# Retention slots of a two-layer decoder step: key transposes and the sample tokens' matvecs moved from the slot's begin into the middle of its weight chunk

## The chip, the cores and the metric

The kernel runs on one NeuronCore of a Trainium2 chip. The metric is the device time of one execution in microseconds (us), as the median of several executions. The engines are TensorE (PE, with its weight loads shown apart as PEld), VectorE (DVE), ScalarE (ACT), GpSimd (POOL) and SyncE (SP), which issues the weight loads from HBM. A row's line, such as L1725, is a line of the kernel before.

## What is computed

A decoder step of two layers for 256 prompt tokens and 8 sample tokens (264 columns, T, in all), in float32. Each layer runs a gated short convolution and a retention branch beside each other, then a dense (layer 0) or a mixture-of-experts (layer 1) channel mixer. Retention, for each of 4 heads, in the form that matters here (q, k, v of 128 rows):

```python
scores = jnp.einsum('blhd,bmhd->bhlm', q, k) * decay[None]
intra = jnp.einsum('bhlm,bmhe->blhe', scores, v)
inter = jnp.einsum('blhd,bhde->blhe', q, state) * q_dec[None, :, :, None]
new_state = jnp.exp(L * log_gamma)[None, :, None, None] * state + jnp.einsum(
    'blhd,blhe->bhde', k * k_dec[None, :, :, None], v)
return intra + inter, new_state
...
a = (cb * conv_out) @ w_conv_out
r = (jax.nn.silu(g.astype(jnp.float32)) * o).astype(xn.dtype) @ w_ret_out
m = jax.nn.sigmoid(ga) * a + jax.nn.sigmoid(gr) * r
return m @ w_o, new_buf, new_state
```

The prompt has no old state; each sample token has its own, of 128 x 128 for each head.

## The kernel before

**Weight chunks.** All weights stream through one ring as chunks of 128 x 2048 floats. SP loads a chunk into `raw` (6 buffers) when the chunk six before it has been cast. ACT writes its rounded half `whi` (L792, 3 buffers) when the PE has begun the chunk behind the one whose buffer it takes, in a slot the slot's own chunk (`chunk_begun`), DVE writes the rest `wlo = raw - whi` (L1246) and releases SP. The PE forms a product as three matmuls (`whi*xh`, `whi*xl`, `wlo*xh`; L1725, L1728, L1729). In the stage at hand a chunk gives 4 output tiles of 12 matmuls (conv) or 2 tiles of 24 (gate), 48 matmuls in all. A tile lies in one of 3 PSUM banks (`RING`): the PE may start tile p when DVE has taken tile p-3 (`tile_taken`; L1429 for conv tiles, L1287 for gate tiles).

**Retention slots.** Behind the last input chunk a layer has ten slots (`for s in range(SLOTS)` on PE, ACT and DVE). Slot s handles a piece of the retention of head s (or s-1, s-2) and then one weight chunk: 2 conv chunks, then 8 gate chunks. In slot s the PE does in this order:

1. slots 1 to 4, head s-1: the outer product of the sample tokens' keys and values for 4 tokens, `outer(0)` (L1822, into bank 7); the prompt's state (L1827) and outputs (L1830, L1831; bank 5); `outer(1)` for the other 4 tokens. It waits for the tiles `ktok`, `kst` and `vd` of head s-1 (`ktok_ready`, `kst_ready`, `vtok_ready`), and `outer(1)` for the first half of the state update (`s_new`), since both use bank 7.
2. slots 0 to 3: two 128 x 128 transposes of the keys and one of the sample keys (L1841, L1842; bank 3). Slots 2 to 5: the 8 matvecs of the sample tokens of head s-2 with their new state (L1848, shown as 16 instructions). `bank3_ready` follows, once a slot.
3. slots 0 to 3: the transposes of the values (L1853, L1854) and the scores (L1855, L1856).
4. the slot's chunk (`chunk`).

Slots 6 to 8 have the normalization of the outputs in place of 1 to 3.

**ACT in a slot:** on `bank3_ready` the copies `ktok` (two, L854), `kst` and `kraw` (L856, L857), and the sample outputs (L860); the prompt's state and outputs (L863, L864); then the cast of a chunk two ahead (L792); from slot 3 on the sigmoids of two gate tiles of the slot before (L847, with a table load in slots 3 and 5), in slot 4 also a silu (L876).

**DVE in a slot:** `state(0)` (L1380; it waits for `outer(0)` and for the loaded old state, `s_in`); copies of the values (L1386, L1387, L1392), the rest of `kst` (L1390), the block-diagonal `vd` (L1396), the decayed scores (L1399, L1400), `state(1)` (L1380), the cast `wlo` (L1246), in slots 3 to 6 the gating of two tiles with ACT's sigmoids (`gated`, L1372), and last the takes of the slot's tiles.

**POOL:** the samples' old states lie in two buffers `St`. POOL stores head h's new state and then, for heads 2 and 3, loads the old state into a free buffer (L532) when `bank3_ready` says that slot h's matvecs are through with it.

Of the kernel before, what the change touches and what calls it, by code (L numbers as in the profile page):

```python
# [34 lines left out]
SEQ = 256  # L35
NB = 8
# [109 lines left out]
def program(nc, A, O):  # L146
# [4 lines left out]
    with es:  # L151
# [634 lines left out]
        def _(act):  # L786
# [37 lines left out]
            for l in range(DEPTH):  # L824
# [22 lines left out]
                        nc.scalar.activation(g, g, ACT.Sigmoid).then_inc(gsig, 1)  # L847

                for s in range(SLOTS):
                    if s < NH:  # L850
                        h = s
                        act.wait_ge(bank3_ready, 6 * l + s + 1)
                        for i in range(2):
                            nc.scalar.activation(ktok[:, 128 * i:128 * i + 128], PS[:, 3, 128 * i:128 * i + 128], ACT.Copy,  # L854
                                                 scale=kd[:, 2 * h + i:2 * h + i + 1]).then_inc(ktok_ready, 1)
                        nc.scalar.activation(kst, PS[0:24, 3, 256:384], ACT.Copy, scale=m1).then_inc(ktok_ready, 1)  # L856
                        nc.scalar.activation(kraw, PS[0:24, 3, 256:384], ACT.Copy).then_inc(kraw_ready, 1)  # L857
                    if 2 <= s < NH + 2:
                        act.wait_ge(bank3_ready, 6 * l + s + 1)
                        nc.scalar.activation(Qt[:, s - 2, SEQ:T], PS[:, 3, 384:384 + NB], ACT.Copy).then_inc(os_taken, 1)  # L860
                    if 1 <= s < NH + 1:
                        act.wait_ge(o_ready, 4 * l + s)
                        nc.scalar.activation(so[:, s - 1, :], PS[:, 5, 384:512], ACT.Copy).then_inc(so_ready, 1)  # L863
                        nc.scalar.activation(Qt[:, s - 1, 0:SEQ], PS[:, 5, 0:SEQ], ACT.Copy).then_inc(o_taken, 1)  # L864
                    if s == 6:
                        act.wait_ge(cent_ready, l + 1)
                        nc.scalar.activation(Qt, PS[:, 4:8, 0:T], ACT.Copy).then_inc(oc_ready, 1)
                    if s == 7:
                        act.wait_ge(var_ready, l + 1)
                        nc.scalar.activation(gstat[:, 0, :], PS[0:TT, 3, 0:12], ACT.Sqrt, bias=epsb[0:TT, :],  # L870
                                             scale=1.0 / DK).then_inc(groot_ready, 1)
                    cast(slot_chunk(b, s) + AHEAD)
                    if s > 2:
                        sigmoids(s - 1)
                    if s == 4:
                        nc.scalar.activation(Gt, Gt, ACT.Silu).then_inc(gsilu_ready, 1)  # L876
                    if s == 8:
                        act.wait_ge(r32, l + 1)
                        nc.scalar.activation(fr[:, 0:4 * T], Qt, ACT.Copy).then_inc(r_hi, 1)
# [353 lines left out]
        def _(dve):  # L1233
# [74 lines left out]
            for l in range(DEPTH):  # L1308
# [63 lines left out]
                        v.tensor_tensor(zt[:, n, :], zt[:, n, :], gate_tile(n), ALU.mult).then_inc(a_gated, 1)  # L1372

                for s in range(SLOTS):
                    if 1 <= s < NH + 1:
                        r = 4 * l + s - 1
                        def state(hf):
# [6 lines left out]
                    if s < NH:  # L1384
                        dve.wait_ge(vT_ready, 4 * l + s + 1)
                        v.tensor_copy(vtok, PS[:, 6, 0:256]).then_inc(vtok_ready, 1)  # L1386
                        v.tensor_scalar(vst, PS[0:24, 6, 256:384], m2, None, ALU.mult).then_inc(vst_ready, 1)  # L1387
                        dve.wait_ge(ktok_ready, 12 * l + 3 * s + 3)
                        dve.wait_ge(kraw_ready, 4 * l + s + 1)
                        v.tensor_tensor(kst, kraw, kst.bitcast(F32), ALU.subtract).then_inc(kst_ready, 1)  # L1390
                        dve.wait_ge(vst_ready, 8 * l + 2 * s + 1)
                        v.scalar_tensor_tensor(vst, PS[0:24, 6, 256:384], float(DK ** -0.5), vst.bitcast(F32),  # L1392
                                               ALU.mult, ALU.subtract).then_inc(vst_ready, 1)
                        dve.wait_ge(vst_ready, 8 * l + 2 * s + 2)
                        dve.wait_ge(kst_ready, 4 * l + s + 1)
                        v.tensor_tensor(vd, vst.bitcast(F32).unsqueeze(1).to_broadcast([24, 8, 128]),  # L1396
                                        eye24.unsqueeze(2).to_broadcast([24, 8, 128]), ALU.mult).then_inc(vtok_ready, 1)
                        dve.wait_ge(score_ready, 4 * l + s + 1)
                        v.tensor_tensor(sc[:, 0:256], PS[:, 4, 0:256], dec[:, s, :], ALU.mult).then_inc(sc_ready, 1)  # L1399
                        v.tensor_tensor(sc[:, 256:384], PS[:, 4, 256:384], dec[:, s, 0:128], ALU.mult).then_inc(sc_ready, 1)  # L1400
# [24 lines left out]
                    if s < 2:  # L1425
                        for j in range(4 * s, 4 * s + 4):
                            p = t["conv"] + j
                            dve.wait_ge(tile_ready, p + 1)
                            v.tensor_copy(zt[:, j, :], PS[:, p % RING, 0:T]).then_inc(tile_taken, 1)  # L1429
                    else:  # L1430
                        for n in (2 * s - 4, 2 * s - 3):
                            take(t["gate"] + n, gate_tile(n), rstd[:, :])

                def m_rest(j):
                    dve.wait_ge(m_hi, 8 * l + j + 1)
# [274 lines left out]
        def _(pe):  # L1710
# [17 lines left out]
                mm(out, wh, al, start=False, stop=False)  # L1728
                return mm(out, wl, ah, start=False, stop=last)  # L1729

            def chunk(c, p, nk, nt, ah, al, turns=0, turns12=0, each=None, norm=None):

                ready(c, turns)
                W = nt * 128
                for n in range(nt):
# [7 lines left out]
                    ins.then_inc(tile_ready, 1)  # L1743
                    if n == 0 and norm is not None:
                        stat(norm)

            def stat(norm):

# [29 lines left out]
            for l in range(DEPTH):  # L1778
# [26 lines left out]
                pe.wait_ge(kv_rows, 2 * l + 2)  # L1805
                pe.wait_ge(tile_taken, t["in"] + 24)
                for s in range(SLOTS):
                    if s > 0 and s <= NH:

                        h, r = s - 1, 4 * l + s - 1  # L1810
# [22 lines left out]

                        pe.wait_ge(s_new, 2 * r + 1)
                        outer(1)
                    if s < NH + 2:
                        if s > 2:
                            pe.wait_ge(os_taken, 4 * l + s - 2)
                        if s < NH:
                            for i in range(2):  # L1840
                                nc.tensor.transpose(PS[:, 3, 128 * i:128 * i + 128], Kt[:, s, 128 * i:128 * i + 128], ident)  # L1841
                            ins = nc.tensor.transpose(PS[0:24, 3, 256:384], sq[:, 24 * s:24 * s + 24], ident)  # L1842
                        if s >= 2:

                            r = 4 * l + s - 2
                            pe.wait_ge(s_new, 2 * r + 2)
                            for i in range(NB):
                                ins = mm(PS[:, 3, 384 + i:385 + i], St[r % 2][:, 128 * i:128 * i + 128],  # L1848
                                         Qt[:, s - 2, SEQ + i:SEQ + i + 1], start=True, stop=True)
                        ins.then_inc(bank3_ready, 1)  # L1850
                    if s < NH:
                        for i in range(2):
                            nc.tensor.transpose(PS[:, 6, 128 * i:128 * i + 128], Vt[:, s, 128 * i:128 * i + 128], ident)  # L1853
# [24 lines left out]
                    if s < 2:  # L1878
                        if s == 0:
                            pe.wait_ge(a_lo, l + 1)  # L1880
                        chunk(b["conv"] + s, t["conv"] + 4 * s, 4, 4, frt[:, 0:4, :], frt[:, 4:8, :])
                    else:
                        chunk(b["gate"] + s - 2, t["gate"] + 2 * s - 4, 8, 2, xht, xlt)
                pe.wait_ge(r_lo, l + 1)
                for i in range(2):
                    chunk(b["ret"] + i, t["ret"] + 4 * i, 4, 4, frt[:, 0:4, :], frt[:, 4:8, :])
# [65 lines left out]
```

## Time and profile before

| | us |
|---|---|
| median of 3 executions | 1825.89 |
| lowest, highest | 1825.65, 1826.80 |
| the profiled execution: device time | 1828.56 |
| the profiled execution: span of the core | 1826.80 |
| slots 0 to 9, layer 0 (first key transpose to last gate tile) | about 111 to 201 |
| slots 0 to 9, layer 1 | about 604 to 695 |

The profile page gives each engine's busy time, the chain of work that ended last, and groups of instructions. The timeline lists an engine's instructions in order of time: start, duration, engine, line, operation, and in brackets how long the engine had been idle before and what released it. Consecutive equal instructions are merged, with the time from the first's start to the last's end. A PE matmul's duration includes its latency, so in a stream the starts tell the pace.

### The profile page before, as it was taken

How to read it: one execution, taken by the hardware profiler on the slowest of the kernel's cores; microseconds unless marked ns; L12 is line 12 of the kernel's file. 1: busy time of each engine (PE TensorE's matmuls, PEld its weight loads, DVE VectorE, ACT ScalarE, POOL GpSimd, SP SyncE). 2: the span in 40 equal slices, each digit the busy share in tenths (PEclk: the TensorE clock that was granted, in tenths of full speed). 3: DMA queues.
4: the chain of work that ended last, by engine and by line, in shares of the span. 5: the costliest groups of instructions: out<-in, count | busy, mean ns of one | idle time of the engine just before them, and what ended most of it. 6: DMA issues, size and time to landing. Idle time of an engine off the chain costs nothing.

```text
span 1826.8 us, 27978 instructions
## 1 busy us (share of the span) xinstructions
PE 1765.9 (97%) x10593; PEld 1568.5 (86%) x10593; DVE 1440.2 (79%) x1341; ACT 1072.5 (59%) x877; POOL 148.2 (8%) x157
## 2 busy tenths in 40 slices
PE   5999999999989999899999999999999999999987
PEld 5989999999989899778888888888888888888866
DVE  5786676556678766588898988988988989989886
ACT  3334544444443255477777777777777777767753
POOL 3112220000231123100000000000000000000002
PEclk9999999999999999799999999999999999999998
DMA  9555455655654545299999999999999999999950
GB/s 294 190 167 171 157 175 167 196 187 144 206 184 163 173 150 168 71 357 374 330 359 349 350 356 335 362 366 333 353 372 330 357 345 348 364 333 361 369 200 25
DMA packets 278305, 483.71 MB, mean 265 GB/s; under 512 B 7951, under 2 KB 126943, under 8 KB 278235
## 3 DMA queue, kind: packets, MB, share of 16 engines
q1 hardware_dynamic: 275159, 473.07, 74.4%
q0 software_dynamic: 2880, 9.56, 1.9%
q8 instruction: 49, 0.80, 0.2%
q10 hardware_dynamic: 196, 0.11, 0.0%
q14 instruction: 21, 0.17, 0.0%
HBM read 476.83 MB, written 5.87 MB: 264 GB/s over the span
## 4 chain that ended last, share of the span: by engine, by line
PE 88%; DVE 8%; ACT 2%; issue 1%; DMA 1%; POOL 0%; SPq 0%; DVEq 0%; ACTq 0%; POOLq 0%
PE PS L1579 11%; PE PS L1583 11%; PE PS L1582 11%; PE PS L1725 10%; PE PS L1728 10%; PE PS L1729 10%; PE PS L1597 6%; PE PS L1600 6%; PE PS L1601 6%; DVE wlo L1246 3%; PE PS L1559 1%; PE PS L1609 1%; ACT whi L792 1%; DMA raw<-in_w_in 1%; PE PS L1848 1%
## 5 line engine op out<-in xcount | busy, mean ns | idle before, releaser
L1246 DVE TENSOR_TENSOR wlo<-raw,whi 128x2048 fp32r<-128x2048 f32 x450 | 1037.6, 2309 | 248.1 <-ACT whi L792 243.5
L792 ACT ACTIVATE whi<-raw 128x2048 fp32r<-128x2048 f32 x450 | 862.5, 1919 | 413.4 <-PE PS L1725 190.1
L1725 PE MATMUL PS<-xh,whi 128*128 128x264 f32 x1280 | 372.3, 291 | 20.4 <-DVE xl L1252 16.9
L1728 PE MATMUL PS<-xl,whi 128*128 128x264 f32 x1280 | 367.4, 287 | 0.0
L1729 PE MATMUL PS<-xh,wlo 128*128 128x264 f32 x1280 | 366.8, 287 | 0.0
L1579 PE MATMUL PS<-whi,xh 128*128 128x512 f32 x896 | 354.0, 395 | 0.9 <-DVE wlo L1246 0.9
L1583 PE MATMUL PS<-whi,xl 128*128 128x512 f32 x896 | 350.2, 391 | 0.0
L1582 PE MATMUL PS<-wlo,xh 128*128 128x512 f32 x896 | 349.6, 390 | 0.0
L1725 PEld LDWEIGHTS PS<-xh,whi 128*128 128x128 f32 x1280 | 245.7, 192 | 22.9 <-issue 8.3
L1728 PEld LDWEIGHTS PS<-xl,whi 128*128 128x128 f32 x1280 | 246.2, 192 | 0.3
L1729 PEld LDWEIGHTS PS<-xh,wlo 128*128 128x128 f32 x1280 | 244.8, 191 | 0.0
L1583 PEld LDWEIGHTS PS<-whi,xl 128*128 128x128 f32 x896 | 168.5, 188 | 36.2
L1579 PEld LDWEIGHTS PS<-whi,xh 128*128 128x128 f32 x896 | 168.7, 188 | 35.2 <-issue 1.3
L1582 PEld LDWEIGHTS PS<-wlo,xh 128*128 128x128 f32 x896 | 168.9, 188 | 32.9
L1597 PE MATMUL PS<-whi,fr 128*128 128x512 f32 x448 | 179.1, 400 | 2.1 <-DVE fr L1139 2.1
L1600 PE MATMUL PS<-wlo,fr 128*128 128x512 f32 x448 | 177.7, 397 | 0.0
L1601 PE MATMUL PS<-whi,fr 128*128 128x512 f32 x448 | 177.1, 395 | 0.0
L1725 PE MATMUL PS<-fr,whi 128*128 128x264 f32 x480 | 137.4, 286 | 3.9 <-DVE z L1429 3.9
L1729 PE MATMUL PS<-fr,wlo 128*128 128x264 f32 x480 | 136.2, 284 | 0.0
L1728 PE MATMUL PS<-fr,whi 128*128 128x264 f32 x480 | 135.9, 283 | 0.0
L498 POOL TENSOR_TENSOR sacc<-x 128x264 f32<-128x264 f32 x7 | 4.8, 682 | 1299.0 <-DVEq L1224 1035.2
L1597 PEld LDWEIGHTS PS<-whi,fr 128*128 128x128 f32 x448 | 84.4, 188 | 22.1 <-DVE wlo L1246 2.3
(268 smaller groups left out, 1706.5 us busy)
## 6 DMA issues: line engine op xcount, KB each, us to landing
raw<-in_w_exp_gu SPq DMA_DIRECT2D x224, 1024.0 KB, 5.4
raw<-in_w_exp_down SPq DMA_DIRECT2D x112, 1024.0 KB, 5.2
raw<-in_w_in SPq DMA_DIRECT2D x44, 1024.0 KB, 5.1
raw<-in_w_dense_gu SPq DMA_DIRECT2D x28, 1024.0 KB, 5.1
raw<-in_w_dense_down SPq DMA_DIRECT2D x16, 896.0 KB, 5.1
raw<-in_w_o SPq DMA_DIRECT2D x8, 1024.0 KB, 5.1
raw<-in_w_ple_gate SPq DMA_DIRECT2D x8, 1024.0 KB, 5.9
scr<-in_state_ret POOLq DMA_DIRECT2D x8, 512.0 KB, 4.8
```

The lines of the kernel that those rows point to most:

```text
L792: nc.scalar.activation(whi[:, c % CAST, :], raw[:, c % RAW, :], ACT.Copy).then_inc(hi_done, 1)
L1246: v.tensor_tensor(wlo[:, c % CAST, :], raw[:, c % RAW, :], whi[:, c % CAST, :].bitcast(F32), ALU.subtract).then_inc(lo_done, 1)
L1559: ins = mm(PS[:, 5 + h, :], sel[:, i, :], tok[:, i, 512 * h:512 * h + 512], start=n == 0 and i == 0, stop=n == 1 and i == 2)
L1579: ins = mm(PS[:, bank, :], gh[:, 128 * kk:128 * kk + 128], wh, start=kk == 0, stop=False)
L1582: mm(PS[:, bank, :], gh[:, 128 * kk:128 * kk + 128], wl, start=False, stop=False)
L1583: ins = mm(PS[:, bank, :], gl[:, 128 * kk:128 * kk + 128], wh, start=False, stop=kk == 7)
L1597: ins = mm(PS[:, h, :], ah, wh, start=first and kk == 0, stop=False)
L1600: mm(PS[:, h, :], ah, wl, start=False, stop=False)
L1601: ins = mm(PS[:, h, :], al, wh, start=False, stop=last and kk == 3)
L1725: ins = mm(out, wh, ah, start=first, stop=False)
L1728: mm(out, wh, al, start=False, stop=False)
L1729: return mm(out, wl, ah, start=False, stop=last)
```

## The change

The key transposes and the matvecs (item 2 above) become a function that `chunk` calls in the middle of the slot's chunk: after tile 1 of 4, or tile 0 of 2. ACT's copies that wait for `bank3_ready` stand behind its cast and ahead of its sigmoids. DVE's `kst` and `vd` become `rows(s)` and stand behind the take of the chunk's middle tile. No instruction is added or taken away; POOL's program is the same.

```diff
@@ ACT, slot s
-                    if s < NH:
-                        h = s
-                        act.wait_ge(bank3_ready, 6 * l + s + 1)
...
                     cast(slot_chunk(b, s) + AHEAD)
+                    if s < NH:
+                        h = s
+                        act.wait_ge(bank3_ready, 6 * l + s + 1)
+                        for i in range(2):
+                            nc.scalar.activation(ktok[:, 128 * i:128 * i + 128], PS[:, 3, 128 * i:128 * i + 128], ACT.Copy,
+                                                 scale=kd[:, 2 * h + i:2 * h + i + 1]).then_inc(ktok_ready, 1)
+                        nc.scalar.activation(kst, PS[0:24, 3, 256:384], ACT.Copy, scale=m1).then_inc(ktok_ready, 1)
+                        nc.scalar.activation(kraw, PS[0:24, 3, 256:384], ACT.Copy).then_inc(kraw_ready, 1)
+                    if 2 <= s < NH + 2:
+                        act.wait_ge(bank3_ready, 6 * l + s + 1)
+                        nc.scalar.activation(Qt[:, s - 2, SEQ:T], PS[:, 3, 384:384 + NB], ACT.Copy).then_inc(os_taken, 1)
                     if s > 2:
                         sigmoids(s - 1)
@@ DVE, slot s
+                    def rows(s):
+
+                        dve.wait_ge(ktok_ready, 12 * l + 3 * s + 3)
+                        dve.wait_ge(kraw_ready, 4 * l + s + 1)
+                        v.tensor_tensor(kst, kraw, kst.bitcast(F32), ALU.subtract).then_inc(kst_ready, 1)
+                        dve.wait_ge(vst_ready, 8 * l + 2 * s + 2)
+                        dve.wait_ge(kst_ready, 4 * l + s + 1)
+                        v.tensor_tensor(vd, vst.bitcast(F32).unsqueeze(1).to_broadcast([24, 8, 128]),
+                                        eye24.unsqueeze(2).to_broadcast([24, 8, 128]), ALU.mult).then_inc(vtok_ready, 1)
...
                             v.tensor_copy(zt[:, j, :], PS[:, p % RING, 0:T]).then_inc(tile_taken, 1)
+                            if j % 4 == 1:
+                                rows(s)
                     else:
                         for n in (2 * s - 4, 2 * s - 3):
                             take(t["gate"] + n, gate_tile(n), rstd[:, :])
+                            if n % 2 == 0 and s < NH:
+                                rows(s)
@@ PE, chunk
                     if n == 0 and norm is not None:
                         stat(norm)
+                    if n == nt // 2 - 1 and between is not None:
+                        between()
@@ PE, slot s
-                        chunk(b["conv"] + s, t["conv"] + 4 * s, 4, 4, frt[:, 0:4, :], frt[:, 4:8, :])
+                        chunk(b["conv"] + s, t["conv"] + 4 * s, 4, 4, frt[:, 0:4, :], frt[:, 4:8, :],
+                              between=keys_and_samples)
                     else:
-                        chunk(b["gate"] + s - 2, t["gate"] + 2 * s - 4, 8, 2, xht, xlt)
+                        chunk(b["gate"] + s - 2, t["gate"] + 2 * s - 4, 8, 2, xht, xlt, between=keys_and_samples)
```

ACT, layer 0, slot 3, before: the copies of head 3 (`ktok` twice, `kst`, `kraw`, the sample outputs), the prompt's copies, the cast, the sigmoids.

```order
L854 ACTIVATE scr<-PS,con 128x128 [waits bank3_ready]
L854 ACTIVATE scr<-PS,con 128x128
L856 ACTIVATE fr<-PS,con 24x128
L857 ACTIVATE scr<-PS 24x128
L860 ACTIVATE z<-PS 128x8 [waits bank3_ready]
L863 ACTIVATE scr<-PS 128x128 [waits o_ready]
L864 ACTIVATE z<-PS 128x256
L792 ACTIVATE whi<-raw 128x2048 [waits chunk_begun,raw_landed1]
L847 ACT_TABLE_LOAD
L847 ACTIVATE z<-z 128x264 [waits tile_taken] x2
```

The same slot on ACT now (L866 to L872 are the old L854 to L860, L852 and L853 the old L863 and L864):

```order
L852 ACTIVATE scr<-PS 128x128 [waits o_ready]
L853 ACTIVATE z<-PS 128x256
L792 ACTIVATE whi<-raw 128x2048 [waits chunk_begun,raw_landed1]
L866 ACTIVATE scr<-PS,con 128x128 [waits bank3_ready]
L866 ACTIVATE scr<-PS,con 128x128
L868 ACTIVATE fr<-PS,con 24x128
L869 ACTIVATE scr<-PS 24x128
L872 ACTIVATE z<-PS 128x8 [waits bank3_ready]
L847 ACT_TABLE_LOAD
L847 ACTIVATE z<-z 128x264 [waits tile_taken] x2
```

The five copies that wait for the PE's bank 3 now stand between the cast and the table load with its sigmoids.

DVE, layer 0, from slot 3's `kst` to slot 4's `state(0)`, before:

```order
L1390 TENSOR_TENSOR fr<-scr,fr 24x128 [waits kraw_ready,ktok_ready]
L1392 SCALAR_TENSOR_TENSOR wr<-PS,wr 24x128 [waits vst_ready]
L1396 TENSOR_TENSOR fr<-wr,con 24x1024 [waits kst_ready,vst_ready]
L1399 TENSOR_TENSOR scr<-PS,con 128x256 [waits score_ready]
L1400 TENSOR_TENSOR scr<-PS,con 128x128
L1380 SCALAR_TENSOR_TENSOR scr<-scr,PS 128x512 [waits kv_outer]
L1246 TENSOR_TENSOR wlo<-raw,whi 128x2048 [waits hi_done]
L1372 TENSOR_TENSOR z<-z 128x264 [waits gsig] x2
L1287 TENSOR_TENSOR z<-PS,rstd 128x264 [waits tile_ready] x2
L1380 SCALAR_TENSOR_TENSOR scr<-scr,PS 128x512 [waits kv_outer,s_in1]
```

The same stretch on DVE now (L1379 is `kst`, L1382 `vd`, L1390 the state update):

```order
L1399 SCALAR_TENSOR_TENSOR wr<-PS,wr 24x128 [waits vst_ready]
L1402 TENSOR_TENSOR scr<-PS,con 128x256 [waits score_ready]
L1403 TENSOR_TENSOR scr<-PS,con 128x128
L1390 SCALAR_TENSOR_TENSOR scr<-scr,PS 128x512 [waits kv_outer]
L1246 TENSOR_TENSOR wlo<-raw,whi 128x2048 [waits hi_done]
L1372 TENSOR_TENSOR z<-z 128x264 [waits gsig] x2
L1287 TENSOR_TENSOR z<-PS,rstd 128x264 [waits tile_ready]
L1379 TENSOR_TENSOR fr<-scr,fr 24x128 [waits kraw_ready,ktok_ready]
L1382 TENSOR_TENSOR fr<-wr,con 24x1024 [waits kst_ready,vst_ready]
L1287 TENSOR_TENSOR z<-PS,rstd 128x264 [waits tile_ready]
L1390 SCALAR_TENSOR_TENSOR scr<-scr,PS 128x512 [waits kv_outer,s_in1]
```

`kst` and `vd` of the slot now stand behind the cast, the gating with the sigmoids and the first take.

## Rows read from the trace of the kernel before

**Rows 1.** The page: busy time and share of each engine; the ending chain.

```profile
PE 1765.9 (97%) x10593; PEld 1568.5 (86%) x10593; DVE 1440.2 (79%) x1341; ACT 1072.5 (59%) x877; POOL 148.2 (8%) x157
...
PE 88%; DVE 8%; ACT 2%; issue 1%; DMA 1%; POOL 0%; SPq 0%; DVEq 0%; ACTq 0%; POOLq 0%
```

**Rows 2.** Timeline, PE's weight loads, layer 0: the idle times in slots 0 and 1.

```profile
118.16 0.19 PEld L1725 LDWEIGHTS PS<-fr,whi 128*128 128x128 f32 x1 [0.87 <-DVE z L1429]
...
129.12 0.19 PEld L1725 LDWEIGHTS PS<-fr,whi 128*128 128x128 f32 x1 [1.47 <-DVE z L1429]
```

**Rows 3.** Timeline, PE, layer 0: slot 2 ahead of its chunk, and slot 3's begin.

```profile
130.77 0.50 PE L1822 MATMUL PS<-fr 24*128 24x512 f32 x1
...
132.49 0.49 PE L1822 MATMUL PS<-fr 24*128 24x512 f32 x1
132.91 0.44 PE L1841 MATMUL PS<-con,z 128*128 128x128 f32 x2
...
133.30 1.84 PE L1848 MATMUL PS<-z,scr 128*128 128x1 f32 x16
135.00 0.42 PE L1853 MATMUL PS<-con,z 128*128 128x128 f32 x2
...
135.94 0.37 PE L1725 MATMUL PS<-xh,whi 128*128 128x264 f32 x1
...
141.91 0.50 PE L1822 MATMUL PS<-fr 24*128 24x512 f32 x1
```

**Rows 4.** Timeline, DVE, layer 0, slot 1: `kst`, `vd`, the cast, three takes.

```profile
123.66 0.28 DVE L1390 TENSOR_TENSOR fr<-scr,fr 24x128 fp32r<-24x128 f32 x1
...
124.18 1.21 DVE L1396 TENSOR_TENSOR fr<-wr,con 24x1024 fp32r<-24x1024 f32 x1
...
126.45 2.27 DVE L1246 TENSOR_TENSOR wlo<-raw,whi 128x2048 fp32r<-128x2048 f32 x1
128.65 1.09 DVE L1429 COPY z<-PS 128x264 f32<-128x264 f32 x3
```

**Rows 5.** Timeline, ACT, layer 0: the cast of slot 1, then slot 3.

```profile
123.89 1.90 ACT L792 ACTIVATE whi<-raw 128x2048 fp32r<-128x2048 f32 x1
...
146.32 0.63 ACT L854 ACTIVATE scr<-PS,con 128x128 f32<-128x128 f32 x2 [7.85 <-PE PS L1848]
...
147.25 0.15 ACT L860 ACTIVATE z<-PS 128x8 f32<-128x8 f32 x1
...
149.65 1.28 ACT L847 ACT_TABLE_LOAD   x1
150.94 0.74 ACT L847 ACTIVATE z<-z 128x264 f32<-128x264 f32 x2
```

**Rows 6.** Timeline, POOL, layer 0: loads of the old states of heads 2 and 3.

```profile
135.74 0.91 POOL L532 DMA_DIRECT2D scr<-in_state_ret  x1 [7.98 <-PE PS L1848]
```

**Rows 7.** All eight instructions of L532: their transfers.

```profile
DMA to landing us min/median/max: 4.5/4.8/9.0
```

**Rows 8.** Timeline, DVE, layer 0: slot 3's `state(0)`; the gating in slot 3.

```profile
142.51 0.69 DVE L1380 SCALAR_TENSOR_TENSOR scr<-scr,PS 128x512 f32<-128x512 f32 x1
...
152.43 0.76 DVE L1372 TENSOR_TENSOR z<-z 128x264 f32<-128x264 f32 x2
```

**Rows 9.** Windows: busy time (instructions) of each engine, granted clock, DMA share, GB/s.

```profile
154.00:157.00 3.00, 3.00 (x23) 2.58 (x23) 1.16 (x2) 0.00 (x0) 0.70 (x1) 1.00 0.94 336
157.00:162.00 5.00, 5.00 (x30) 5.00 (x30) 2.36 (x2) 4.78 (x8) 0.96 (x2) 0.66 0.56 167
158.00:159.00 1.00, 1.00 (x7) 1.00 (x6) 0.00 (x0) 1.00 (x1) 0.59 (x1) 0.50 1.00 295
164.00:169.00 5.00, 5.00 (x45) 5.00 (x44) 0.86 (x2) 2.54 (x3) 0.00 (x0) 1.00 0.49 196
...
638.00:643.00 5.00, 5.00 (x30) 4.75 (x30) 3.49 (x9) 3.51 (x9) 0.89 (x1) 0.66 0.43 123
652.00:657.00 5.00, 5.00 (x31) 5.00 (x30) 3.21 (x4) 4.75 (x5) 0.75 (x1) 0.66 0.53 157
```

**Rows 10.** Timeline, PE, layer 0: the matvecs of slots 4 and 5.

```profile
155.21 1.95 PE L1848 MATMUL PS<-z,scr 128*128 128x1 f32 x16
...
164.45 1.84 PE L1848 MATMUL PS<-z,scr 128*128 128x1 f32 x16
```

More of the change, by code:

```diff
@@ L849, in _ @@
                 for s in range(SLOTS):
-                    if s < NH:
-                        h = s
-                        act.wait_ge(bank3_ready, 6 * l + s + 1)
[L853 to L860, printed above, removed]
                     if 1 <= s < NH + 1:
@@ L1387, in _ @@
                         v.tensor_scalar(vst, PS[0:24, 6, 256:384], m2, None, ALU.mult).then_inc(vst_ready, 1)
-                        dve.wait_ge(ktok_ready, 12 * l + 3 * s + 3)
-                        dve.wait_ge(kraw_ready, 4 * l + s + 1)
-                        v.tensor_tensor(kst, kraw, kst.bitcast(F32), ALU.subtract).then_inc(kst_ready, 1)
                         dve.wait_ge(vst_ready, 8 * l + 2 * s + 1)
@@ L1393, in _ @@
                                                ALU.mult, ALU.subtract).then_inc(vst_ready, 1)
[L1394 to L1397, printed above, removed]
                         dve.wait_ge(score_ready, 4 * l + s + 1)
@@ L1729, in three, with chunk @@
                 return mm(out, wl, ah, start=False, stop=last)
-            def chunk(c, p, nk, nt, ah, al, turns=0, turns12=0, each=None, norm=None):
+            def chunk(c, p, nk, nt, ah, al, turns=0, turns12=0, each=None, norm=None, between=None):
                 ready(c, turns)
@@ L1807, in _, with keys_and_samples @@
                 for s in range(SLOTS):
+                    def keys_and_samples():
+                        if s >= NH + 2:
+                            return
+                        if s > 2:
+                            pe.wait_ge(os_taken, 4 * l + s - 2)
+                        if s < NH:
+                            for i in range(2):
+                                nc.tensor.transpose(PS[:, 3, 128 * i:128 * i + 128], Kt[:, s, 128 * i:128 * i + 128], ident)
+                            ins = nc.tensor.transpose(PS[0:24, 3, 256:384], sq[:, 24 * s:24 * s + 24], ident)
+                        if s >= 2:
+                            r = 4 * l + s - 2
+                            pe.wait_ge(s_new, 2 * r + 2)
+                            for i in range(NB):
+                                ins = mm(PS[:, 3, 384 + i:385 + i], St[r % 2][:, 128 * i:128 * i + 128],
+                                         Qt[:, s - 2, SEQ + i:SEQ + i + 1], start=True, stop=True)
+                        ins.then_inc(bank3_ready, 1)
                     if s > 0 and s <= NH:
@@ L1835, in _ @@
                         outer(1)
[L1836 to L1850, printed above, removed]
                     if s < NH:
```

## The prediction

> **What bounds the kernel now.** I read the page first: TensorE is busy for 97% of the span and carries 88% of the chain that ended last [rows 1]. A change pays only where it takes something out of the PE's own time, and costs wherever it makes the PE wait. Next I read the timelines of the retention slots, since nothing else is touched. What the reader is to see there is that the PE hardly ever waits. In slots 0 and 1 it waits for DVE's takes of a conv tile, 0.87 and 1.47 us by its weight loads [rows 2], of which some 0.8 and 1.4 are real against a stream. Layer 1 shows the same two gaps, and slots 2 to 9 show none that matters. Last I read the windows for the clock. Three times, once in layer 0 and twice in layer 1, the granted clock is 0.66 over 5 us, and inside it is 0.50, the level of 1.2 GHz instead of 2.4; each costs 5 x 0.34 = 1.7 us, 5.1 in all [rows 9].
>
> **The pace of a slot.** From [rows 3], slot 2: `outer(0)` to the first key transpose 132.91 - 130.77 = 2.14 us, with `outer(1)` 1.72 behind `outer(0)`. Key transposes and matvecs take 135.00 - 132.91 = 2.09, values and scores 0.94, the chunk 141.91 - 135.94 = 5.97, so half a chunk 3.0. The last matvec ends at 135.14, 0.14 behind the moment T at which the PE goes on. Now T is the begin of the chunk's second half, and the next slot's `outer(0)` could run at T + 3.0. That is all the cover that the moved work has. Before, a whole chunk, values and scores lay behind it: 6.9 us.
>
> **The removed wait: slots 0 and 1.** In slot 1 DVE casts at 126.45 because `kst` and `vd` stand ahead of it [rows 4]; without them (0.3 + 1.2) it could start at 124.95, but it also needs ACT's cast, which ended at 123.89 + 1.90 = 125.79 [rows 5]. ACT loses the copies ahead of it and the chunk begins 0.3 earlier, so I put that end at 125.25. The takes come 1.2 us earlier, and the fourth tile starts 1.2 earlier than 129.12. Then comes a small new wait. Casting 2.2, two takes 0.7, `kst` 0.3 and `vd` 1.2 end at 129.65, while the PE would be at `outer(0)` at 129.57. The gain is 130.77 - 129.7 = 1.1 us. In slot 0 ACT's cast already sets DVE's, to within 0.2 us, and `vd` takes that back: nothing. The price of splitting a chunk is one more restart, since a first matmul shows 0.37 instead of 0.28 [rows 3]: 0.1 in each of slots 2 to 4. Slots 0 and 5 only exchange one seam for another.
>
> **New wait A: the state load, slot 3.** POOL's program is unchanged, but its load of head 2's state waits for `bank3_ready` of slot 2, which now comes in mid-chunk. In the trace the issue follows the end of the last matvec by 135.74 - 135.14 = 0.60 us [rows 3, 6]. The landing takes 4.5 to 9.0 us over eight loads, median 4.8 [rows 7]. Before, `state(0)` started at 142.51 [rows 8], 6.8 us behind the issue, and the load was hidden. Now the issue is at T + 0.74 and with 4.8 the state is there at T + 5.54. `state(0)` takes 0.69, so `outer(1)`, which needs bank 7 back, runs at T + 6.25 instead of T + 3.0 + 1.72: a wait of 1.5 us. With 4.5 it is 1.2, with 9.0 it is 5.7. The load now also overlaps a weight load: the casts (0.4 + 1.90 + 2.27 behind the chunk's begin) release SP some 1.2 us ahead of it. I take a landing of 5.2, near the median, since 9.0 belongs to the crowd of first loads: 1.9 us. Queued behind `state(0)` on DVE are the value copies and the cast, but the PE needs these only later. Head 3's load has the same delay in slot 4, where it hides behind wait B.
>
> The Trainium skill, page "DMA: Bandwidth & Descriptors", section "Queues, rings and completion order", says that each DMA engine serves its queue rows in turn, packet by packet; by this the state load would share with the weight load instead of queueing behind it, so its 4.8 would stretch but not wait out the whole weight load. Nothing in the trace of before shows that overlap inside the slots, and the sum above keeps both ends from rows.
>
> **New wait B: `vd`, slot 4.** On ACT the sigmoids stand behind the copies that wait for the PE's middle. On DVE the gating needs the sigmoids and stands ahead of the take and of `rows(3)`, and `outer(0)` of slot 4 needs `vd`. Step by step from T: ACT starts at T + 0.2, reaches the end of its small copies 1.0 later (146.32 to 147.25, and 0.1), loads the table 1.3, runs two sigmoids 0.74 [rows 5]: T + 3.25. The second gating and the take need 0.34 each (152.43, 0.76 for two [rows 8]), `kst` 0.3, `vd` 1.2 [rows 4]: T + 5.5. The PE is there at T + 3.0, so it waits 2.5 us (2.2 to 2.8 with DVE's overlaps read either way). In slots 4 and 5 the sigmoids are late too, but no `vd` follows, and the ring asks for the late take only a chunk later: nothing. In slot 2 there are no sigmoids and the chain is T + 0.2 + 0.95 + 0.3 + 1.2 = T + 2.7, just under 3.0: nothing, or 0.2.
>
> **Sum.** Each layer: -1.1 + 0.3 + 1.9 + 2.5 = +3.6 us. Both: +7.2.
>
> **The clock.** The three drops come right behind matvecs (16 instructions of one column, 1.95 us [rows 10]) that stood next to other thin work. In slot 5, where matvecs stand between two chunks, the clock stays at 1.00 from 164 to 169 [rows 9]. The change makes that the rule, which speaks for fewer drops. But it puts idle stretches of 1.9 and 2.5 us into the PE's work, four in all. I take two drops after in place of three: -1.7 us. The Trainium skill, page "TensorE: Matmul & The Clock Gate", section "HAM oscillation — how this bites in real kernels", names idle time between bursts as what costs the clock; the PE was busy for 3.00 of the 3 us ahead of a drop here [rows 9], so the trace shows that busy time alone does not protect it. [...]
>
> **The number.** +7.2 - 1.7 = +5.5 us. Against the profiled execution of 1828.56 (a span of 1826.80 and 1.8 around it) that gives 1834.1; this execution lay 2.7 above the median of 1825.89, so the median goes to 1831.4.
>
> **Rivals.**
> - *The clock holds.* No drop is left: +7.2 - 5.1 = +2.1, 1828.0, within the measurement. For it: slot 5. Against: four new idle stretches.
> - *The clock falls more often.* A drop at each new wait: +7.2 + 1.7 = +8.9, 1834.8. For it: the waits stand next to thin work.
> - *The state load crowds with weights.* With the 9.0 of [rows 7] each wait A grows by 3.8: +13.1, 1839.0; with 7.0 it is +9.1, 1835.0. Against: the weight load is ahead of it and partly through.
> - *The moved work hides, so faster.* If the chain from mid-chunk to `vd` closed within 3.0 us in slot 3 too, and the state landed within 4.0 of T, only the gain is left: 2 x (-1.1 + 0.3) = -1.6, and without drops -6.7, 1819.2. It decides at one place, the sigmoids of slot 3: they would have to be done before the copies. The order shows them behind, so this needs a table load that runs while ACT waits, and the load has to be free for DVE. I see little for it.
>
> **How the numbers follow.** Forecast (1829.6 to 1833.4) 0.52; clock holds 0.17; more drops 0.18; crowded load 0.08; faster 0.05. Slower by over 0.2% (3.7 us, about what a measurement tells from no change) is then 0.52 + 0.18 + 0.08 = 0.78, within 0.17, faster 0.05. The range 1827.5 to 1836.0 leaves out the faster case, the lower part of the second, half of the crowded loads and the last of the drops, some 0.17 together.
>
> **What would show it.** In slots 0 and 1 the idle before a conv tile should be under 0.2 us. In slot 3 of each layer `outer(1)` should be idle 1.2 to 2.5 us on DVE's `state(0)`, and that on the load. In slot 4 `outer(0)` should be idle about 2.5 us on `vd`, with ACT's table load standing behind the sample copy in mid-chunk. In slot 2 the gap at `outer(0)` of slot 3 should be under 0.3. I am wrong if `outer(0)` of slot 4 starts within 1 us of the chunk's end, if the old states land earlier than DVE asks for them, or if the clock drops number none or more than four.

## The result, and the profile after

| | before | after |
|---|---|---|
| median of 4 executions, us | 1826.35 | 1846.08 |
| lowest, highest | 1825.65, 1827.91 | 1841.81, 1847.64 |
| ratio, 95% interval | | 1.0103 (1.0084 to 1.0122) |
| profiled execution: time, span | 1828.56, 1826.8 | 1841.81, 1840.0 |
| mean granted clock | 0.984 | 0.983; the other three 0.981, 0.979, 0.979 |

The change costs 19.7 us, where 5.5 were forecast and 10 were the end of the range. The direction was right, the size was not.

The page of after: the busy line, and the ending chain by engine. Against [rows 1] the PE has 3.5 us more busy time in a span 13.2 us longer; the rest is idle.

```profile
PE 1769.4 (96%) x10593; PEld 1572.6 (85%) x10593; DVE 1440.8 (78%) x1341; ACT 1073.8 (58%) x877; POOL 148.0 (8%) x157
...
PE 87%; DVE 7%; ACT 2%; DMA 2%; issue 1%; POOL 0%; SPq 0%; DVEq 0%; ACTq 0%; POOLq 0%
```

The timeline of the PE, layer 0: the outer products of slots 1 to 4 (slots 3 and 4 with both), in brackets the idle time before each. L1850 is the old L1822.

```profile
119.83 0.47 PE L1850 MATMUL PS<-fr 24*128 24x512 f32 x1 [0.32 <-DVE fr L1382]
...
130.01 0.46 PE L1850 MATMUL PS<-fr 24*128 24x512 f32 x1 [0.28 <-issue]
...
141.19 0.48 PE L1850 MATMUL PS<-fr 24*128 24x512 f32 x1
...
146.35 0.50 PE L1850 MATMUL PS<-fr 24*128 24x512 f32 x1 [3.38 <-DVE scr L1390]
...
160.17 0.47 PE L1850 MATMUL PS<-fr 24*128 24x512 f32 x1 [2.70 <-issue]
...
162.43 0.79 PE L1850 MATMUL PS<-fr 24*128 24x512 f32 x1
```

Both forecast waits are there, in the words of the prediction: wait A (for the loaded state) ahead of 146.35 and wait B (for `vd`) ahead of 160.17. "Issue" names no releaser, but the rows of DVE below show it. Layer 1 shows the same two:

```profile
648.20 0.50 PE L1850 MATMUL PS<-fr 24*128 24x512 f32 x1 [3.16 <-DVE scr L1390]
...
662.03 0.46 PE L1850 MATMUL PS<-fr 24*128 24x512 f32 x1 [2.69 <-issue]
```

**Wait A.** POOL's and DVE's timelines, layer 0: the load of head 2's state (L532), the store of head 1's (L569), `state(0)` (L1390). Before, the load was issued at 135.74 [rows 6] and `state(0)` did not wait [rows 8].

```profile
138.83 0.91 POOL L532 DMA_DIRECT2D scr<-in_state_ret  x1 [12.96 <-PE PS L1832]
139.73 0.89 POOL L569 DMA_DIRECT2D out_ret_sample<-scr  x1
...
145.61 0.69 DVE L1390 SCALAR_TENSOR_TENSOR scr<-scr,PS 128x512 f32<-128x512 f32 x1 [3.89 <-DMA scr<-in_state_ret]
```

From issue to use are 145.61 - 138.83 = 6.8 us, where I had taken 5.2. The loads as a group (before: [rows 7]) and SP's queue, where slot 2's weight load goes out 1.0 us ahead of the state load:

```profile
DMA to landing us min/median/max: 4.9/6.1/9.1
...
L400 SPq DMA_DIRECT2D raw<-in_w_ret_out x1: 368/368/368, 137.8 to 137.8; - x1
```

**Wait B.** ACT and DVE, layer 0, slot 3: ACT's copies and sigmoids, then on DVE the gating (L1372), `kst` and `vd` (L1382), which ends at 159.96. The PE goes on at 160.17.

```profile
155.42 0.15 ACT L872 ACTIVATE z<-PS 128x8 f32<-128x8 f32 x1
155.58 1.28 ACT L847 ACT_TABLE_LOAD   x1
156.88 0.74 ACT L847 ACTIVATE z<-z 128x264 f32<-128x264 f32 x2
...
157.34 0.78 DVE L1372 TENSOR_TENSOR z<-z 128x264 f32<-128x264 f32 x2 [4.54 <-ACT z L847]
158.03 0.43 DVE L1287 TENSOR_TENSOR z<-PS,rstd 128x264 f32<-128x264 f32 x1
158.37 0.27 DVE L1379 TENSOR_TENSOR fr<-scr,fr 24x128 fp32r<-24x128 f32 x1
158.75 1.21 DVE L1382 TENSOR_TENSOR fr<-wr,con 24x1024 fp32r<-24x1024 f32 x1
```

**The ring waits** of [rows 2] are gone down to 0.37 us by the weight loads:

```profile
128.01 0.19 PEld L1732 LDWEIGHTS PS<-fr,whi 128*128 128x128 f32 x1 [0.37 <-DVE z L1432]
```

**The clock.** Windows, columns as in [rows 9]; the last column but two is the granted clock, 0.50 being 1.2 GHz. The first window holds the end of wait A and what follows: the clock is at the lower level for 3.4 us of it, from about 147.6 on. Wait B falls into the second window, at full clock; right behind it the clock is at the lower level for about 7 us.

```profile
146.00:152.00 6.00, 5.65 (x30) 5.33 (x31) 3.89 (x8) 1.91 (x1) 0.00 (x0) 0.72 0.01 2
158.00:161.00 3.00, 0.83 (x4) 0.61 (x5) 2.45 (x6) 0.00 (x0) 0.00 (x0) 1.00 0.85 300
161.00:164.00 3.00, 3.00 (x12) 2.16 (x11) 1.13 (x2) 0.72 (x3) 0.00 (x0) 0.54 0.00 1
164.00:168.00 4.00, 4.00 (x20) 4.00 (x20) 2.22 (x1) 1.74 (x1) 1.64 (x2) 0.50 0.54 158
```

The clock makes the executions differ, so I part each span into two. Span x mean clock is about what the span would be at full clock, and span x (1 - mean clock) is what the clock took. For this profile: 1840.0 x 0.983 = 1808.7 and 31.3; for before (1826.8 x 0.984) 1797.6 and 29.2. The third decimal of the clock is worth 1.8 us, so only medians over runs are used below. By them the kernel before has 1797 and 27.4 (over 13 to 15 executions), the changed one 1807.6 and 36.9: **of the 19.7 us about 10.6 are waits, less the small gain, and about 9 are clock.** Of these 9 the windows find 5.1 in the slots: there the clock took 10.2 us in the profiled execution and 5.1 in that of before. Where the other 4 fall is not shown: outside the slots the profiled execution of before lost 25 us, and two profiled executions of the changed kernel 21 and 27.

### The profile page after: what moved, and what is told of

It is laid out like the page before. It is cut to its first block, busy times and chain, and to the rows that moved or that the text cites. A ratio compares the mean times of both kernels' runs of the same rounds, so it can differ in the third digit from the quotient of the medians.

```text
span 1840.0 us, 27978 instructions
## 1 busy us (share of the span) xinstructions
PE 1769.4 (96%) x10593; PEld 1572.6 (85%) x10593; DVE 1440.8 (78%) x1341; ACT 1073.8 (58%) x877; POOL 148.0 (8%) x157
## 4 chain that ended last, share of the span: by engine, by line
PE 87%; DVE 7%; ACT 2%; DMA 2%; issue 1%; POOL 0%; SPq 0%; DVEq 0%; ACTq 0%; POOLq 0%
PE PS L1586 11%; PE PS L1590 11%; PE PS L1589 11%; PE PS L1732 10%; PE PS L1735 10%; PE PS L1736 10%; PE PS L1604 6%; PE PS L1607 6%; PE PS L1608 6%; DVE wlo L1246 3%; PE PS L1566 1%; ACT whi L792 1%; PE PS L1616 1%; DMA raw<-in_w_in 1%; PE PS L1832 1%
```

## The experiments

| kernel | median, us | ratio to before (95%) | at full clock | clock took | in slots 0 to 9, profiled execution | waits at outer products of slots 3 and 4, us a layer |
|---|---|---|---|---|---|---|
| before | 1826.3 to 1827.4 | | 1797 | 27.4 | 5.1 | none |
| after | 1846.08 | 1.0103 (1.0084 to 1.0122) | 1807.6 | 36.9 | 10.2 | A 3.4, 3.2; B 2.7, 2.7 |
| `after2` (the same) | 1845.75 | 1.0101 (1.0086 to 1.0117) | 1808.4 | 35.0 | 10.2 | A 3.6, 3.3; B 2.7, 2.7 |
| `e1_sig` | 1841.66 | 1.0083 (1.0066 to 1.0100) | 1808.3 | 32.2 | 8.5 | 5.7, 4.5 by state loads |
| `e2_mv` | 1845.51 | 1.0103 (1.0086 to 1.0120) | 1801.9 | 42.4 | 13.7 | B 2.8, 2.8 |
| `e3_both` | 1830.32 | 1.0016 (1.0005 to 1.0026) | 1797.3 | 32.9 | 12.0 | none; 1.1 |
| `e4_mvonly` | 1846.97 | 1.0111 (1.0094 to 1.0128) | 1811.1 | 35.1 | 8.5 | 7.2, 5.9 by state loads |
| `e5_pool` | 1842.37 | 1.0084 (1.0069 to 1.0100) | 1807.4 | 33.1 | 8.5 | A 2.6, 2.9; B 2.7, 2.7 |
| `e6_fill` | 1837.53 | 1.0063 (1.0048 to 1.0078) | 1809.0 | 27.5 | 3.4 | filled |
| `e7_two` | 1823.63 | 0.9986 (0.9977 to 0.9995) | 1796.4 | 25.5 | 0 | none |
| `e7_again` (the same) | 1823.71 | 0.9989 (0.9980 to 0.9998) | 1796.3 | 25.5 | 5.1 | none |
| `e8_late` | 1848.18 | 1.0121 (1.0106 to 1.0137) | 1808.5 | 37.8 | 13.7 | 5.2, 5.2 by state loads |
| `e9_hold` | 1837.96 | 1.0065 (1.0049 to 1.0080) | 1804.6 | 32.1 | 6.8 | A 1.4, 1.3; B 2.7, 2.7 |

The last column but one sums 1 - granted clock over windows of 1 us, for the profiled execution alone; "at full clock" and "clock took" are medians over all executions. The kernels ran on several chips, each beside the kernel before (1826.3 to 1827.4).

Theory: two waits cost the time, as forecast, A because the state load starts late and B because `vd` stands behind late sigmoids; rival: the split chunks themselves, or the clock alone. The first four kernels take these apart.

**Sigmoids first.** In ACT's program of the changed kernel:

```diff
                     cast(slot_chunk(b, s) + AHEAD)
+                    if s > 2:
+                        sigmoids(s - 1)
                     if s < NH:
...
-                    if s > 2:
-                        sigmoids(s - 1)
```

> The changed kernel with one thing undone: on ACT the sigmoids of a slot stand directly behind the cast again, ahead of the copies that wait for the PE's middle. Two-waits theory: the 2.7 us at outer(0) of slot 4 goes in both layers (under 0.3 left), the 3.3 us at outer(1) of slot 3 stays, and the time falls by 5.4 us and by one or two clock drops of 1.7 each: 1837 to 1841 from 1846. Rival (thin work in mid-chunk costs clock by itself): the wait goes but the drops stay as many, 1841 or more.

Wait B is gone: `outer(0)` of slot 4 has no idle time. But the PE then waits at `outer(1)` of slot 4 for head 3's state, 2.48 us in layer 0:

```profile
145.87 0.49 PE L1850 MATMUL PS<-fr 24*128 24x512 f32 x1 [3.20 <-DVE scr L1390]
...
161.23 0.79 PE L1850 MATMUL PS<-fr 24*128 24x512 f32 x1 [2.48 <-DVE scr L1390]
```

So B had hidden a second wait of A's kind. Taking B away alone shortens what the PE waits in slot 4 only from 2.7 us to 2.5 and 1.7 in the two layers, too little to show at full clock (1808.3 against 1807.6 and 1808.4). The 4 us by which the median is lower are clock. The expected 5.4 us less missed, since it left the second wait out.

**Matvecs back at the slot's begin**, with a semaphore of their own (`mv_ready`) for ACT's sample copy and POOL's load; keys stay in mid-chunk.

```diff
+                    samples()          # matvecs, then_inc(mv_ready, 1)
                     if s < NH:
                         for i in range(2):
                             nc.tensor.transpose(PS[:, 6, ...
-                                  between=keys_and_samples)
+                                  between=keys)
@@ POOL, load_state
-                        pool.wait_ge(bank3_ready, ...)
+                        pool.wait_ge(mv_ready, 4 * l + h - 1)
```

> The changed kernel with the matvecs and the sample copy back at the slot's begin with a semaphore of their own, so that POOL loads the old states as early as before; key transposes and their copies stay in mid-chunk. Two-waits theory: the 3.3 us at outer(1) of slot 3 goes in both layers, the landing falls from 6.8 to under 5.2 us, the 2.7 us at slot 4 stays: 6.6 us less and one or two drops fewer, 1836 to 1840. Rival (the state load is late for another reason, crowding alone): the wait stays above 1.5 us.

Wait A is gone in both layers and B stays:

```profile
158.05 0.46 PE L1855 MATMUL PS<-fr 24*128 24x512 f32 x1 [2.77 <-issue]
```

At full clock that saves 6 us, where 6.6 were expected. The time missed its 1836 to 1840: it is that of the changed kernel, since the clock takes 42.4 us instead of 35 to 37. One drop of it stands where neither before nor after has one, in slot 2 behind the matvecs, with the PE busy throughout (the same window is at 1.00 in both others):

```profile
134.00:140.00 6.00, 6.00 (x39) 5.87 (x39) 3.29 (x7) 2.53 (x4) 1.79 (x2) 0.72 0.38 103
```

**Both of these edits.**

> The changed kernel with both undone: matvecs at the slot's begin, sigmoids directly behind the cast; only key transposes, their ACT copies, kst and vd are in mid-chunk. Two-waits theory: nothing of the loss is left, and the 0.6 us per layer gained in slots 0 and 1 shows: 1824 to 1827. Rival (splitting chunks costs time or clock by itself): 1830 or more.

At full clock it is level with before, 1797.3 against 1797. The median is 2.9 us above before (0.16%), all of it clock (32.9 against 27.4 by medians, 32.0 against 27.9 by means). What remains of the change here, the keys in mid-chunk, costs and gains nothing in work. But the expected 1824 to 1827 missed, and the rival's 1830 or more came out: that splitting the chunks costs clock by itself, some 4 us with the matvecs at the slot's begin, is not ruled out.

**The matvecs alone in mid-chunk,** in the kernel before: the function `samples` above is called between the two tiles of a gate chunk, and the keys stay at the slot's begin.

> The kernel before with only the matvecs and the sample copy moved into mid-chunk; keys, kst and vd at the slot's begin as before. Two-waits theory: one wait only, about 3.3 us at outer(1) of slot 3 per layer, and none at slot 4, so 6.6 us over before and zero to two more clock drops: 1833 to 1836. Rival (matvecs between chunk halves keep the clock up): the drops behind them go, and the time is 1829 or less.

This single move brings the whole loss, +14 us at full clock, where 6.6 were expected: slot 4 waits for its state too, since there is no wait B to hide it. Waits of PE by what ended them, slots of layer 0 (us in total, times, longest):

```profile
PE PS L1825 <- DVE scr L1381: 7.2, 2, 3.8
PE PS L1726 <- DVE z L1430: 1.9, 2, 1.3
```

The first row is `outer(1)` of slots 3 and 4, the second the old ring waits.

**The late load with nothing moved.** In the kernel before, POOL's loads of heads 2 and 3 wait for the slot's first gate tile too:

```diff
                         pool.wait_ge(bank3_ready, ...)
+                        if h >= 2:
+                            pool.wait_ge(tile_ready, TB[l]["gate"] + 2 * h - 3)
```

> The kernel before with a single wait added on POOL: the loads of heads 2 and 3 also wait for the first gate tile of slots 2 and 3, which is the moment that releases them in the changed kernel. No PE, ACT or DVE instruction moves. My theory (the late issue of these loads is the main loss): outer(1) waits about 3.4 us in slot 3 and 2 to 3.5 in slot 4 of each layer, +11 to +13 us, 1838 to 1840 before any change of the clock. Rival (the loss needs the split chunks and the moved matvecs): under +6, 1832 or less.

No instruction of PE, ACT or DVE differs from before, and the loss is as large as the change's: +11.6 at full clock, as expected, +22 in all. The slots shared it otherwise than expected: 1.68 us in slot 3 (expected 3.4) and 3.57 in slot 4. Below are head 2's load with slot 3's `state(0)`, head 3's load with slot 4's, and SP's load of slot 2.

```profile
139.59 0.90 POOL L534 DMA_DIRECT2D scr<-in_state_ret  x1 [11.95 <-PE PS L1731]
140.49 0.89 POOL L571 DMA_DIRECT2D out_ret_sample<-scr  x1
...
144.52 0.69 DVE L1382 SCALAR_TENSOR_TENSOR scr<-scr,PS 128x512 f32<-128x512 f32 x1 [2.19 <-DMA scr<-in_state_ret]
...
154.08 0.88 POOL L534 DMA_DIRECT2D scr<-in_state_ret  x1 [12.70 <-PE PS L1731]
...
160.92 0.69 DVE L1382 SCALAR_TENSOR_TENSOR scr<-scr,PS 128x512 f32<-128x512 f32 x1 [4.08 <-DMA scr<-in_state_ret]
...
L400 SPq DMA_DIRECT2D raw<-in_w_ret_out x1: 368/368/368, 141.3 to 141.3; - x1
```

Here head 2's load is used 4.93 us behind its issue, although the store stands right behind it. What differs from the changed kernel is the weight load: 1.7 us behind the state load here, 1.0 us ahead of it there. Head 3's load points the same way: it too has the store behind it, but the weight load goes out at 154.54, 0.5 us behind it, and it is used after 6.84 us. So a weight load need not be ahead to stretch it. That gives two suspects for wait A's size, the store and the weight load.

**The store out of the way.** POOL's order, so that store 1 leaves ahead of load 2:

```diff
-                    if h + 2 < NH:
-                        load_state(h + 2)
+                    if 1 <= h < NH - 1:
+                        load_state(h + 1)
```

> The changed kernel, but POOL issues the store of head 1's state (and of head 2's) ahead of the load of the next head's, so that the store leaves some 4 us before the load and not 0.9 us behind it; nothing else is moved. Store crowds the load: the load, which took about 6.8 us from issue to use (138.83 to 145.61), comes back to about 5.2, outer(1) of slot 3 waits about 1.8 us instead of 3.4 and 3.2, and the time is about 3 us below the changed kernel's (1843), more if head 3's load gains too. Rival, the weight load alone crowds it: the waits stay at 3.2 to 3.4 and the time stays at 1842 to 1847.

```profile
135.53 0.90 POOL L569 DMA_DIRECT2D out_ret_sample<-scr  x1 [9.25 <-DVE scr L1390]
139.25 0.89 POOL L532 DMA_DIRECT2D scr<-in_state_ret  x1 [2.82 <-PE PS L1832]
...
145.30 0.69 DVE L1390 SCALAR_TENSOR_TENSOR scr<-scr,PS 128x512 f32<-128x512 f32 x1 [3.15 <-DMA scr<-in_state_ret]
```

From 6.8 to 6.05 us, not to 5.2, and in layer 1 the wait is 2.9 instead of 3.2: the store is the smaller part. The theory that it alone crowds the load falls.

**The weight load out of the way.** The store stays where the changed kernel has it. SP holds back the loads that the casts of slots 2 and 3 release; each chunk is needed eight chunks later.

```diff
                 for i in range(2):
+                    sp.wait_ge(s_in[i], 16 * (2 * l + 2))
                     load(b["ret"] + i, rows(A["w_ret_out"][l], 4)...
```

> The changed kernel, but SP holds back the weight load that the casts of slots 2 and 3 release (each is needed eight chunks later) until the old state of head 2 or 3 has landed; the store stays where the changed kernel has it, behind the load. The weight load ahead of the state load crowds it (my theory after e5_pool and e8_late: 6.8 us with the weight load 1.0 us ahead and the store behind, 6.0 with the weight load ahead alone, 4.9 with it 1.7 us behind): the state is there 4.6 to 4.9 us behind the issue, outer(1) of slot 3 waits about 1.4 us instead of 3.4 and 3.2, and the time is 3 to 5 us under the changed kernel's beside it. Rival, the landing is long for another reason (the issue from POOL, the store): over 6 us as before, waits of 3 us or more.

```profile
139.30 0.90 POOL L533 DMA_DIRECT2D scr<-in_state_ret  x1 [12.98 <-PE PS L1833]
...
144.07 0.69 DVE L1391 SCALAR_TENSOR_TENSOR scr<-scr,PS 128x512 f32<-128x512 f32 x1 [1.89 <-DMA scr<-in_state_ret]
...
144.82 0.50 PE L1851 MATMUL PS<-fr 24*128 24x512 f32 x1 [1.36 <-DVE scr L1391]
```

4.77 us from issue to use, the median of [rows 7], and a wait of 1.36, with the store still right behind. So the weight load is what stretched it, by 2.0 us. Beside the weight load the store costs 0.75 us (`e5_pool`); without it little is left for the store, since the load lands 4.7 us behind its issue here and 4.5 before. The changed kernel beside it:

> The changed kernel once more, for its time beside e9_hold and for a second profile: the waits at the same places and of the same length (3.2 to 3.4 at outer(1) of slot 3, 2.7 at outer(0) of slot 4), 1841.8 to 1847.6 us, and a clock between 0.979 and 0.983, since the drops of the clock, not the waits, differ from run to run.

The landing and the waits are as expected (one of the repeated kernel's is 3.6, a little over its 3.2 to 3.4). The time is not: `e9_hold` is 7.8 us under the changed kernel, where 3 to 5 were expected. 3.8 of them are at full clock (the waits alone give 2 x 2.1), the rest is clock.

**Idle time and the clock.** The changed kernel with matmuls that nobody reads in the waits:

```diff
+                        def fill(n):
+                            for _ in range(n):
+                                mm(PS[:, 4, 384:512], xht[:, 0, 0:128], xht[:, 1, 0:128], ...)
+                        if s == 4:
+                            pe.wait_ge(sc_ready, 2 * r + 2)
+                            fill(22)
...
+                        if s == 3:
+                            fill(26)
                         pe.wait_ge(s_new, 2 * r + 1)
                         outer(1)
```

> The changed kernel with matmuls that nobody reads (128 columns, into an unused part of a PSUM bank) inside the two waits: 26 ahead of outer(1) of slot 3, 22 ahead of outer(0) of slot 4. The waits cost clock: the PE is no longer idle there, the drops to 0.50 next to them go, some 3 to 5 us of the time with them (about 1841 for the median). Rival, the clock falls for the thin matvecs or for what lies around, not for the idle stretches: the granted clock is as before (0.979 to 0.983) and the time is that of the changed kernel or up to 1 us more.

The work at full clock is unchanged (1809.0), and the clock takes 27.5 us, no more than in the kernel before. Two windows of it: around slot 3's wait, and slot 4's wait with what follows.

```profile
146.00:150.00 4.00, 4.00 (x18) 3.47 (x19) 2.17 (x6) 1.21 (x1) 0.00 (x0) 0.57 0.02 4
158.00:164.00 6.00, 5.71 (x41) 4.94 (x40) 3.05 (x5) 2.30 (x3) 1.15 (x2) 1.00 0.44 153
```

Where the changed kernel's clock fell behind wait B it now holds, in layer 1 too. Behind slot 3's wait it still falls once in each layer; there 0.49 us of idle time were left and thin work stands on both sides. So idle stretches of 2.7 to 3.4 us, 12 us together, cost some 7 to 9 us more through the clock, about twice what was expected: the median is 8.5 us lower with the same waits, and in the slots the clock takes 3.4 us instead of 10.2.

**The part that pays.** The change in slots 0 and 1 alone; from slot 2 on PE, ACT and DVE keep the order of before.

```diff
@@ PE, slot s
+                    if s >= 2:
+                        keys_and_samples()
...
-                        chunk(b["gate"] + s - 2, ..., between=keys_and_samples)
+                        chunk(b["gate"] + s - 2, ...)
```

> The change in slots 0 and 1 alone (key transposes in mid-chunk there, rows behind the second take); slots 2 to 5 keep the order of the kernel before, so that matvecs, state loads and sigmoids are where they were. My theory: what the change gained is the ring waits of slots 0 and 1, 0.6 us a layer in the trace of after; the time is 1.2 us under the kernel before, 1825.2 against 1826.4, if the clock is the same. Rival: the small wait for vd that now ends slot 1 and the clock take it back: 1826 to 1828.

> The kernel of e7_two once more, on whatever chip it meets: 2 to 3 us under the kernel before (e7_two measured 1823.63 against 1826.3), with no drop of the clock in slots 0 to 6. Rival, its lead was luck with the clock: within 1 us of before.

1823.63 and 1823.71, 2.7 and 3.2 us under the kernel before (1.2 were expected at first), with intervals that just leave out 1. Two of the eleven executions of the second lie above every one of before beside them. In its first profile the clock does not fall in the slots at all; the second row is of before:

```profile
111.00:181.00 70.00, 68.63 (x527) 64.16 (x528) 45.88 (x75) 31.36 (x52) 13.73 (x12) 1.00 0.55 168
```

```profile
111.00:181.00 70.00, 67.67 (x507) 63.34 (x507) 43.80 (x69) 29.69 (x50) 13.43 (x13) 0.98 0.50 157
```

In the second profile it does (0.95 and 0.98 over 70 us in the two layers, 5.1 us, as much as before), so that expectation missed. At full clock the lead is 0.5 to 0.9 us, near the 0.8 that the traces give (2 x 0.4: from the first key or value transpose to slot 6's first matmul 58.54 and 58.49 us, against 58.9 of before less its clock). The rest is clock, 1 to 3 us by the means, and no run shows that it will always be there. This version beats both kernels, the one before by little more than 0.1%.

## Why the prediction was wrong in size, point by point

The stage's length, for the table: from the first transpose of slot 0 to the first matmul of slot 6, layer 0, PE, of before and of after.

```profile
111.39 0.41 PE L1841 MATMUL PS<-con,z 128*128 128x128 f32 x2 [0.43 <-issue]
...
172.04 1.95 PE L1862 MATMUL PS<-z,con 128*128 128x264 f32 x8
```

```profile
111.18 0.41 PE L1866 MATMUL PS<-con,z 128*128 128x128 f32 x2 [0.43 <-issue]
...
180.65 1.95 PE L1875 MATMUL PS<-z,con 128*128 128x264 f32 x8
```

Before it is 60.65 us, of which the clock took 1.7 [rows 9]: 58.9. After it is 69.47; the profile has the lower level for 10.2 us of it, which cost 5.1: 64.4, 5.4 more. In the same way layer 1 gives 5.2. To slot 3's `outer(0)` it was 141.91 - 111.39 = 30.52 and is 141.19 - 111.18 = 30.01.

| us a layer, at full clock | forecast | layer 0, layer 1 |
|---|---|---|
| slots 0 to 2: ring waits, restart | -1.0 | -0.5, -0.5 |
| wait A | +1.9 | +3.4, +3.2 |
| wait B | +2.5 | +2.7, +2.7 |
| the rest (restarts; measured: what remains) | +0.2 | -0.2, -0.2 |
| sum | +3.6 | +5.4, +5.2 |

- **Where the time goes: right.** Both waits are at the instructions named, with the releasers named, and nothing else is late by more than 0.4 us. A single edit takes away each of them (`e2_mv`, `e1_sig`). Nothing of what was to show it wrong came (the four drops are at its limit), but the wait at `outer(1)` left its 1.2 to 2.5 us.
- **Wait A: mechanism right, size wrong.** The failed step is "I take a landing of 5.2, near the median". It saw that the load would overlap a weight load, and bounded the overlap by 9.0, but took a value near the landings of a load that overlaps nothing. It measured 6.8. Without the weight load it is 4.8 (`e9_hold`), without the store 6.05 (`e5_pool`): the weight load is worth 2.0 us, and the store, whose overlap I had not seen, 0.75 of these beside it. POOL's program is unchanged, but the load that came 3 us later closed the gap to the store (139.45 before, 139.73 after). With the landing of `e9_hold` the changed kernel loses 1804.6 - 1797 = 7.6 us at full clock, where the sum said 7.2; that this is so near is partly luck, since a wait A of 1.3 to 1.4 instead of 1.9 makes up for the half of the gain that is missing. By the Trainium skill, page "DMA: Bandwidth & Descriptors", section "Queues, rings and completion order", the load shares the engines with what other queues hold; the trace agrees: the state load was stretched, but did not wait for the weight load to end. That one landed at 143.0 (137.8 and 5.2 to landing), and 4.8 more would be 147.8, where the state was used at 145.61.
- **Wait B: right**, 2.7 against 2.5, link by link. That head 3's load "hides behind wait B" was right too (`e1_sig` uncovered it), and it makes B worthless to mend alone.
- **The gain: half of it.** `vd` ended slot 1 as foreseen (PE at 130.01, forecast 129.7 to go on), and slot 1 is 0.8 us shorter (130.01 - 119.83 = 10.18 against 10.95) where 1.1 were forecast. But in slot 0, which I put at nothing, `vd` takes 0.2 us that were not there: slot 1's `outer(0)` waits 0.32 us.
- **The clock: wrong sign.** Forecast -1.7, measured +8 to +9 over whole executions, +5.1 in the slots of both profiles. The failed step is "I take two drops after in place of three". It named four idle stretches as a danger and gave them no price. `e6_fill` prices them at 7 to 9 us with the waits left as they are. This is the largest single miss. Here the page "TensorE: Matmul & The Clock Gate" of the Trainium skill, section "HAM oscillation — how this bites in real kernels", pointed the right way: waits between bursts of matmuls are what it names, though it has longer ones in mind than these. The trace agrees for the new waits, behind each of which the clock fell. It also shows a drop with no idle time ahead of it (`e2_mv`, 134 to 140), so waits are not the only cause.
- **The rival that the clock falls more** had the right sign and the right number, four drops, one behind each new wait. But it priced each at 1.7 us: those behind wait A cost that, those behind wait B 3.4, so it had +1.7 where the slots show +5.1. The rival of a crowded state load had the right mechanism at 8 in 100. Both came true together, and no case had them together.

What stays open: why the clock takes 5 us more in `e3_both` than in before, with the same work and nearly no idle time, and 42 us in `e2_mv`, which idles less than the changed kernel (2.8 us a layer at its waits against 5.9 to 6.1). In the slots their profiled executions lost 12.0 and 13.7 us, and both have a drop in slot 2, with the PE busy. Thin work stands at other places in both; no run here separates that. Nor does a run show where the changed kernel loses the 4 us of clock that its slots don't account for.

## What to carry to other kernels

A semaphore that an edit moves may be read by an engine whose program the edit doesn't touch: follow each reader, and for a DMA look at what is in flight at its new time, on every queue, since its landing time was measured in its old company. An idle stretch of the PE costs its length and may cost more behind it: here 12 us of them took another 7 to 9 through the clock, so put that into the sum and not only into the rivals. If an edit helps in two slots and hurts in four, make it in the two.

## What the runs showed that I had not expected

- A state load of 512 KB is used 4.8 us behind its issue with the store right behind it and no weight load in flight, 4.9 with the store and a weight load of 1 MB 1.7 us later, and 6.8 with the store and the weight load either 1.0 us ahead or 0.5 us behind. With the weight load 1.0 us ahead and no store it is 6.05.
- The PE idled 2.2 of 3 us at full clock (the window 158:161 of after); the clock fell to 0.50 only when it had gone on, over 7 us in which it was busy throughout.
- `e3_both` and `e7_two` have the same work at full clock to within 1 us, and differ by 6.7 us in time (on two chips; against before beside them by 5.6).
